# Border of two sublayers: `sqsum` statistics inside the last group, last chunk squared in two halves

## Chip, core and metric

The kernel runs on one core of a Trainium2 chip. The metric is the device time of one execution in microseconds; lower is better. Engines are named as in the profile: TensorE is PE (matmuls) and PEld (weight loads), VectorE is DVE, ScalarE is ACT, GpSimd is POOL, SyncE is SP, which issues the DMAs.

## What is computed

An encoder trunk of two layers on 512 tokens of width 1024, in float32. Every layer has an FFN, a token mixer (latent attention "MLA" in layer 0, gated recurrence "HGRN" in layer 1) and another FFN, so there are six sublayers. Each has an RMS norm at its entry and one at its end, before the residual addition:

```python
for l in range(DEPTH):
    g = norm_gains[l]
    x = x + 0.5 * rmsnorm(swiglu(rmsnorm(x, g[0]), ffn_w_in[l, 0], ffn_w_out[l, 0]), g[1])
    h = rmsnorm(x, g[2])
    m = mla(h, ...) if l % 2 == 0 else hgrn2(h, ...)
    x = x + rmsnorm(m, g[3])
    x = x + 0.5 * rmsnorm(swiglu(rmsnorm(x, g[4]), ffn_w_in[l, 1], ffn_w_out[l, 1]), g[5])
# rmsnorm(x, gain) = x * rsqrt(mean(x * x, axis=-1) + 1e-6) * gain
```

## The kernel before

All activations lie transposed: 1024 features as `KB` = 8 chunks of 128 partitions, 512 tokens as columns. A weight tile is 128x1024 (eight blocks of 128x128). Products are made exact enough by splitting both sides into a high and a low part: ScalarE rounds a tile (`w_hi`, L1339), GpSimd (L528) or VectorE (L1809) takes the rest (`w_lo`), and `mm3` issues three 128x512 matmuls for each block (L578 to L580). A group is one output chunk: 8 blocks for the up projection, the MLA output and the HGRN output, 22 blocks (`FB`) for the down projection of an FFN, each block three wide matmuls into one PSUM bank. Four weight slots form a ring; SP loads a slot (L453) when TensorE has released it through `w_free`.

The order of the work on each engine is written out by hand; waits are on semaphores and every engine runs its instructions in order. A sublayer ends with eight groups, output chunks 0 to 7 (`output_projection` on VectorE and ScalarE). For chunks 0 to 6, VectorE copies the group from PSUM into `y` (L1874), ScalarE squares the copy into `sq` (L1352, `square_y`), and VectorE adds the square to `sqsum` (L1882, L1885; signal `sq_added`). The last chunk is squared by ScalarE straight from PSUM (same line), and VectorE copies it only after that.

Then comes the border, of which there are six, the one after the last sublayer included. `post_statistics` on TensorE (L648) waits for seven `sq_added`, multiplies the four 128-token blocks of `sqsum` with a column of ones into PSUM bank `STAT` (L652; the first one releases the last weight slot, `close`), waits for the last square (`sq_ready`, L656) and adds the four products of `sq` (L658). ScalarE takes the root (L1357), VectorE the reciprocal (L1776), TensorE widens it over the partitions (L681), and VectorE normalises chunk after chunk and adds it to x (L1789, L1794); ScalarE forms `xg_hi` of each chunk (L1382), with which the next sublayer's first matmuls begin (L724). `keep_clock` (L675) fills waits with matmuls whose result is not used. At the FFN's end ScalarE runs one weight split (L1339) between the last square and the root, and after the first `xg_hi` it runs the split of the tile whose slot the last group held. At entry, `pre_statistics` (L668) makes four products of the same form as L652 in the middle of a group. TensorE's down projection is a loop of two turns with four groups each (L830).

## Time and profile before

| | us |
|---|---|
| median of 3 runs | 2062.91 (2062.24 to 2064.61) |
| profiled execution, its time | 2064.43 |
| profiled execution, its span | 2062.6 |
| PE busy | 2047.6 (99%) |
| DVE, ACT, POOL busy | 919.6, 713.2, 664.5 |

The span runs from the first to the last instruction of the program. Busy time is the union of the instructions' records; matmul records overlap, so the distance between two starts is the pace, not the length of one. "Idle before" is the time in which an engine stood still ahead of an instruction, with the engine and line that released it.

### The profile page before, as it was taken

What the parts mean: (1) busy time and instruction counts of PE and PEld (TensorE: products, weight loads), DVE (VectorE), ACT (ScalarE), POOL (GpSimd) and SP (SyncE); (2) the same over time, 40 slices, a digit from 0 to 9 for tenths busy, and PEclk for the clock granted to TensorE, in tenths of its full rate; (3) what the DMA queues carried; (4) which work ended last, traced back from release to release, by engine and by line L of the source; (5) the groups of instructions that cost most, each with busy time, mean ns of one, the idle gap of its engine ahead of it and who ended that gap; (6) DMA issues with size and microseconds to landing.
All of it is one profiled execution on the core that took longest, in us unless ns stands there. A gap on an engine that the chain in (4) does not pass through costs nothing.

```text
span 2062.6 us, 28297 instructions
## 1 busy us (share of the span) xinstructions
PE 2047.6 (99%) x11146; PEld 1676.7 (81%) x11146; DVE 919.6 (45%) x1223; ACT 713.2 (35%) x957; POOL 664.5 (32%) x286
## 2 busy tenths in 40 slices
PE   9999999999999999999999999999999999999998
PEld 7888888777888888888888888888888778888886
DVE  5434331668465334115543321466766775343212
ACT  4222232445342222223322222365655542222221
POOL 2444444230224444442444444200000014444442
PEclk9999999999999999999999999999999999999999
DMA  4332333310122323333223333222212122323332
GB/s 154 93 101 92 94 100 92 102 52 1 52 92 83 100 92 97 97 94 99 83 92 101 92 95 96 85 90 76 73 62 66 59 72 93 102 92 97 90 103 77
DMA packets 51634, 179.46 MB, mean 87 GB/s; under 512 B 5728, under 2 KB 5984, under 8 KB 51552
## 3 DMA queue, kind: packets, MB, share of 16 engines
q1 hardware_dynamic: 51552, 178.30, 27.5%
q8 instruction: 59, 0.97, 0.2%
q14 instruction: 23, 0.19, 0.0%
HBM read 176.18 MB, written 2.10 MB: 86 GB/s over the span
## 4 chain that ended last, share of the span: by engine, by line
PE 96%; DVE 2%; ACT 1%; issue 0%; DMA 0%; SPq 0%; DVEq 0%; ACTq 0%
PE psum L578 28%; PE psum L580 27%; PE psum L579 27%; PE psum L724 2%; PE psum L942 1%; PE psum L730 1%; PE psum L725 1%; PE psum L918 1%; PE psum L931 1%; PE psum L1048 1%; PE psum L681 0%; PE psum L750 0%; PE psum L757 0%; PE psum L754 0%; PE psum L1128 0%; PE psum L1085 0%
## 5 line engine op out<-in xcount | busy, mean ns | idle before, releaser
L528 POOL TENSOR_TENSOR w_lo<-raw,w_hi 128x1024 fp32r<-128x1024 f32 (+1 forms) x282 | 664.3, 2357 | 1370.0 <-ACT w_hi L1339 1370.0
L578 PE MATMUL psum<-xg_hi,w_hi 128*128 128x512 f32 x1735 | 688.8, 397 | 2.9 <-DVE xg_lo L2111 2.6
L580 PE MATMUL psum<-xg_hi,w_lo 128*128 128x512 f32 x1735 | 680.9, 392 | 0.0
L579 PE MATMUL psum<-xg_lo,w_hi 128*128 128x512 f32 x1735 | 675.5, 389 | 0.0
L1339 ACT ACTIVATE w_hi<-raw 128x1024 fp32r<-128x1024 f32 (+1 forms) x339 | 350.8, 1037 | 859.6 <-DMA raw<-w_up 471.6
L580 PEld LDWEIGHTS psum<-xg_hi,w_lo 128*128 128x128 f32 x1735 | 326.1, 188 | 75.2
L579 PEld LDWEIGHTS psum<-xg_lo,w_hi 128*128 128x128 f32 x1735 | 326.3, 188 | 70.4
L578 PEld LDWEIGHTS psum<-xg_hi,w_hi 128*128 128x128 f32 x1735 | 326.5, 188 | 69.6 <-DVE xg_lo L2111 2.9
L578 PE MATMUL psum<-hid_hi,w_hi 128*128 128x512 f32 x704 | 274.0, 389 | 0.0
L580 PE MATMUL psum<-hid_hi,w_lo 128*128 128x512 f32 x704 | 273.9, 389 | 0.0
L579 PE MATMUL psum<-hid_lo,w_hi 128*128 128x512 f32 x704 | 273.9, 389 | 0.0
L1853 DVE TENSOR_TENSOR t_b<-psum,r_pre 128x512 f32<-128x512 f32 x100 | 69.1, 691 | 348.3 <-PE psum L580 347.5
L1874 DVE COPY y<-psum 128x512 f32<-128x512 f32 x48 | 33.2, 692 | 402.4 <-PE psum L580 345.5
L578 PEld LDWEIGHTS psum<-hid_hi,w_hi 128*128 128x128 f32 x704 | 132.1, 188 | 27.5
L580 PEld LDWEIGHTS psum<-hid_hi,w_lo 128*128 128x128 f32 x704 | 132.1, 188 | 27.5
L579 PEld LDWEIGHTS psum<-hid_lo,w_hi 128*128 128x128 f32 x704 | 132.1, 188 | 27.5
L1860 DVE TENSOR_TENSOR t_d<-t_c,t_b 128x512 f32<-128x512 f32 x88 | 134.0, 1523 | 17.4 <-ACT t_c L1404 6.2
L1853 DVE TENSOR_TENSOR t_a<-psum,r_pre 128x512 f32<-128x512 f32 x100 | 69.1, 691 | 128.2 <-PE psum L580 107.8
L1404 ACT ACTIVATE t_c<-t_a 128x512 f32<-128x512 f32 x88 | 55.7, 633 | 127.2 <-DVE t_a L1853 127.2
L1809 DVE TENSOR_TENSOR w_lo<-raw,w_hi 128x1024 fp32r<-128x1024 f32 x57 | 69.7, 1223 | 12.6 <-ACT w_hi L1339 11.4
L1864 DVE TENSOR_TENSOR hid_lo<-t_d,hid_hi 128x512 f32 (+1 forms) x88 | 69.3, 788 | 9.4
L1885 DVE TENSOR_TENSOR sqsum<-sqsum,sq 128x512 f32<-128x512 f32 x36 | 43.1, 1198 | 32.5 <-ACT sq L1352 32.5
(233 smaller groups left out, 1595.4 us busy)
## 6 DMA issues: line engine op xcount, KB each, us to landing
raw<-w_up SPq DMA_DIRECT2D x176, 512.0 KB, 3.6
raw<-w_down SPq DMA_DIRECT2D x64, 512.0 KB, 3.5
raw<-w_hgrn SPq DMA_DIRECT2D x48, 512.0 KB, 3.6
raw<-w_down SPq DMA_DIRECT2D x32, 384.0 KB, 3.1
raw<-w_mla SPq DMA_DIRECT2D x19, 512.0 KB, 3.6
xt<-x_t SPq DMA_DIRECT2D x8, 256.0 KB, 6.4
out<-xt SPq DMA_DIRECT2D x8, 256.0 KB, 2.2
sq<-positions SPq DMA_DIRECT2D x1, 256.0 KB, 9.3
```

The costliest lines, as they stand in the source:

```text
L528: pool.tensor_tensor(w_lo[slot][:, 0:n], raw[slot][:, 0:n], w_hi[slot][:, 0:n].bitcast(F32), ALU.subtract).then_inc(w_ready, 1)
L578: first = pe.matmul(ps, w_hi[slot][:, at:at + n], hi, start=start, stop=False)
L579: pe.matmul(ps, w_hi[slot][:, at:at + n], lo, start=False, stop=False)
L580: return first, pe.matmul(ps, w_lo[slot][:, at:at + n], hi, start=False, stop=stop)
L724: first = pe.matmul(banks[g], w_hi[tiles[g]][:, at], xg_hi[:, k, :], start=k == 0, stop=False)
L1339: act.activation(w_hi[slot][:, 0:n], raw[slot][:, 0:n], ACT.Copy).then_inc(hi_made, 1)
L1404: act.activation(t_c[:, :], t_a[:, :], ACT.Silu).then_inc(silu_done, 1)
L1809: dve.tensor_tensor(w_lo[slot][:, :], raw[slot][:, :], w_hi[slot][:, :].bitcast(F32), ALU.subtract).then_inc(lo_made, 1)
L1853: dve.tensor_tensor(dst, bank(), r_pre[:, :], ALU.mult).then_inc(drained, 1)
L1860: dve.tensor_tensor(t_d[:, :], t_c[:, :], t_b[:, :], ALU.mult).then_inc(dve_step, 1)
L1864: dve.tensor_tensor(hid_lo[:, f, :], t_d[:, :], hid_hi[:, f, :].bitcast(F32), ALU.subtract).then_inc(hidden_ready, 1)
L1885: dve.tensor_tensor(sqsum[:, :], sqsum[:, :], src, ALU.add).then_inc(sq_added, 1)
```

## The change

Three edits. The products of `sqsum` leave `post_statistics` and become `sum_statistics`, which TensorE runs inside the last group of each sublayer: ahead of the last block of eight in MLA and HGRN, ahead of block 19 of 22 in an FFN; the wait for `sq_added` goes with them. The last chunk is squared in two instructions of 256 columns, each with its own signal, and the four products of `sq` wait for the first half ahead of the first and for the second half ahead of the third; the last slot is now released by the first of these. To place the products in the last group alone, TensorE's loop over the down projection is written out. VectorE's copy of the last chunk waits for both halves.

```diff
-            def group_into(ps, slot, hi, lo, middle=None, later=None):
+            def group_into(ps, slot, hi, lo, middle=None, later=None, final=None):
                 for k in range(KB):
+                    if final and k == KB - 1:
+                        final()
                     first, last = mm3(ps, (slot, k * P, P), hi[:, k, :], lo[:, k, :], k == 0, k == KB - 1)
...
-            def post_statistics():
+            def sum_statistics():
 
                 pe.wait_ge(sq_added, added.next(KB - 1))
                 for b in range(TB):
-                    first = pe.matmul(psum[:, STAT, b:b + 1], sqsum[:, b * P:(b + 1) * P], ones[:, 0:1],
-                                      start=b == 0, stop=False, skip_group_check=True)
+                    pe.matmul(psum[:, STAT, b:b + 1], sqsum[:, b * P:(b + 1) * P], ones[:, 0:1],
+                              start=b == 0, stop=False, skip_group_check=True)
+
+            def post_statistics():
+
+                for b in range(TB):
                     if b == 0:
-                        close(first)
-                pe.wait_ge(sq_ready, squared.next(KB))
-                for b in range(TB):
+                        pe.wait_ge(sq_ready, squared.next(KB))
+                    elif b == TB // 2:
+                        pe.wait_ge(sq_ready, squared.next())
                     last = pe.matmul(psum[:, STAT, b:b + 1], sq[:, (KB - 1) % 2, b * P:(b + 1) * P], ones[:, 0:1],
                                      start=False, stop=b == TB - 1, skip_group_check=True)
+                    if b == 0:
+                        close(last)
                 last.then_inc(stat_done, 1)
...
-                with loop(pe, KB // 4, (ready, 4 * len(DOWN_PARTS)), (bank_free, 4), stream=stream):
+                for i in range(KB // 4):
                     for j in range(4):
...
+                                if f == FB - 3 and i * 4 + j == KB - 1:
+                                    sum_statistics()
...
-                for _ in range(2, KB):
-                    group_into(open_next(), open_tile(), xg_hi, xg_lo)
+                for j in range(2, KB):
+                    slot = open_tile()
+                    group_into(open_next(), slot, xg_hi, xg_lo, final=sum_statistics if j == KB - 1 else None)
...
-                project(by_dve=False)
+                slot = open_tile()
+                group_into(open_group(LONG_RING), slot, xg_hi, xg_lo, final=sum_statistics)
...
-                    src = psum[:, ends[0], :]
+                    for at in (slice(0, SEQ // 2), slice(SEQ // 2, SEQ)):
+                        act.activation(sq[:, j % 2, at], psum[:, ends[0], at], ACT.Square).then_inc(sq_ready, 1)
+                    return
...
-                        dve.wait_ge(sq_ready, squared.next())
+                        dve.wait_ge(sq_ready, squared.next(2))
```

## Rows read from the trace of the kernel before

**Rows 1.** The page: engines' busy time, and the chain that ended last.
```profile
PE 2047.6 (99%) x11146; PEld 1676.7 (81%) x11146; DVE 919.6 (45%) x1223; ACT 713.2 (35%) x957; POOL 664.5 (32%) x286
PE 96%; DVE 2%; ACT 1%; issue 0%; DMA 0%; SPq 0%; DVEq 0%; ACTq 0%
```

**Rows 2.** Timeline, first border: start us, length us, engine, line, operands, [idle before].
```profile
374.67 0.39 PE L580 MATMUL psum<-hid_hi,w_lo 128*128 128x512 f32 x1
374.67 1.08 PEld L652 LDWEIGHTS psum<-const,sqsum 128*128 128x128 f32 x8
375.15 0.60 ACT L1352 ACTIVATE sq<-psum 128x512 f32<-128x512 f32 x1 [4.80 <-PE psum L580]
375.65 1.05 ACT L1339 ACTIVATE w_hi<-raw 128x1024 fp32r<-128x1024 f32 x1
375.80 1.05 PE L658 MATMUL psum<-const,sq 128*128 128x1 f32 x8
376.89 0.26 ACT L1357 ACTIVATE root<-psum,eps 128x4 f32<-128x4 f32 x1 [0.20 <-PE psum L658]
380.34 1.04 ACT L1339 ACTIVATE w_hi<-raw 128x1024 fp32r<-128x1024 f32 x1
```

**Rows 3.** Timeline, second border, after the MLA layer.
```profile
578.00 0.60 ACT L1352 ACTIVATE sq<-psum 128x512 f32<-128x512 f32 x1 [0.71 <-PE psum L580]
579.74 0.26 ACT L1357 ACTIVATE root<-psum,eps 128x4 f32<-128x4 f32 x1 [1.14 <-PE psum L658]
```

**Rows 4.** Timeline, `pre_statistics` (L668) inside a group at the entry of MLA.
```profile
405.22 0.40 PE L580 MATMUL psum<-xg_hi,w_lo 128*128 128x512 f32 x1
405.45 0.95 PE L668 MATMUL psum<-const,sqsum 128*128 128x1 f32 x8
406.26 0.48 PE L578 MATMUL psum<-xg_hi,w_hi 128*128 128x512 f32 x1
406.58 0.39 PE L579 MATMUL psum<-xg_lo,w_hi 128*128 128x512 f32 x1
```

**Rows 5.** ScalarE, a group by form (busy us, mean ns), and a timeline row.
```profile
L1608 ACT ACTIVATE state<-psum 128x256 f32<-128x256 f32 x8 | 3.1, 383 | 7.7 <-PE psum L1106 7.7
...
1485.16 1.52 ACT L1591 ACTIVATE near<-psum 32x256 f32<-32x256 f32 x4
```

**Rows 6.** Timeline, border after the HGRN layer.
```profile
1676.85 1.34 DVE L1885 TENSOR_TENSOR sqsum<-sqsum,sq 128x512 f32<-128x512 f32 x1 [0.76 <-ACT sq L1352]
1677.26 0.39 PE L578 MATMUL psum<-xg_hi,w_hi 128*128 128x512 f32 x1
1678.24 0.97 PEld L652 LDWEIGHTS psum<-const,sqsum 128*128 128x128 f32 x8 [0.56 <-DVE sqsum L1885]
1678.66 1.28 SPq L453 DMA_DIRECT2D raw<-w_up  x3
1679.16 1.03 PE L658 MATMUL psum<-const,sq 128*128 128x1 f32 x8
1680.23 0.26 ACT L1357 ACTIVATE root<-psum,eps 128x4 f32<-128x4 f32 x1 [1.42 <-PE psum L658]
```

**Rows 7.** Timeline, last addition to `sqsum` in the first FFN and in MLA.
```profile
361.65 1.13 DVE L1885 TENSOR_TENSOR sqsum<-sqsum,sq 128x512 f32<-128x512 f32 x1 [0.76 <-ACT sq L1352]
...
573.96 0.79 DVE L1885 TENSOR_TENSOR sqsum<-sqsum,sq 128x512 f32<-128x512 f32 x1 [0.76 <-ACT sq L1352]
```

**Rows 8.** L453 at the first border: ns min/median/max, first and last start; landing us.
```profile
L453 SPq DMA_DIRECT2D raw<-w_mla x3: 328/430/432, 375.2 to 376.1; - x3
...
DMA to landing us min/median/max: 3.8/4.7/5.5
```

**Rows 9.** Timeline, TensorE at the end of the down loop's first turn.
```profile
314.83 0.39 PE L580 MATMUL psum<-hid_hi,w_lo 128*128 128x512 f32 x1
315.06 0.39 PE L578 MATMUL psum<-hid_hi,w_hi 128*128 128x512 f32 x1
```

**Rows 10.** A stretch: us; busy PE, PEld, DVE, ACT, POOL; PEclk, DMA share, GB/s.
```profile
1618.00:1621.40 3.40, 2.69 (x6) 2.15 (x7) 3.33 (x6) 1.00 (x2) 0.00 (x0) 0.59 0.05 18
```

## Prediction

> **What bounds the kernel now.** I read the page first: TensorE is busy in 99% of the span and the chain that ended last is 96% TensorE [rows 1]. So whatever is added to TensorE's stream counts in full, and other engines count only where TensorE waits for them. That happens at the six borders, where a sublayer's output is normalised and each new chunk of x needs the previous result. The second view is the timeline of the first border [rows 2]. Let A be the start of the squaring of the last chunk there, 375.15. The last wide matmul starts 0.48 before A. The reader should see two things run side by side after it. ScalarE squares 512 columns in 0.60 and the square is usable at 375.75. TensorE meanwhile does the four `sqsum` products (eight passes, since each fp32 product is recorded as two), and these have been issued at 375.75 too (374.67 + 1.08). At 375.80 the four products with `sq` begin, at 376.89 the root. So the `sqsum` products have hardly any price at present: the squaring covers them. From A to the root it is 1.74, at this border, where a weight split stands in between, and at the second, where none does [rows 3].
>
> **The change part by part.** Times are us.
>
> 1. *Four `sqsum` products move into the last group.* The nearest row is the same work in the same place: `pre_statistics` in the middle of a group [rows 4]. Without it a matmul follows every 0.23, so after the L580 at 405.22 an L578 would start at 405.45 and an L579 at 405.68. With the eight passes the L579 starts at 406.58. The cost is 406.58 - 405.68 = 0.90 of TensorE's own time. Ends: 0.81, if only the gap from first pass to next wide matmul is counted (406.26 - 405.45), and 0.90, which I take, as the L578 behind them is itself stretched. Nothing hides it, since the group's end, and A with it, come 0.90 later. I call the new start A'.
>
> The Trainium skill (TensorE: Matmul & The Clock Gate, LDWEIGHTS) gives a weight load 128/1.2 = 107 ns; eight would be an estimated 0.85 by that page, and the sum 0.3 smaller over six borders. The trace measures the pair and decides.
>
> 2. *Squaring in two halves.* No row shows a half square, but ScalarE took 383 ns for 256 columns out of PSUM [rows 5] where 512 took 0.60. So the first half is ready at A' + 0.38 and TensorE starts at A' + 0.43, with the 0.05 between a ScalarE end and TensorE's start that 375.75 to 375.80 shows. The second half: four 256-column reads of PSUM by L1591 took 1.52 together, hence 0.38 each without overlap [rows 5]; it ends at A' + 0.77 and is usable at A' + 0.82. The third product is due at A' + 0.43 + 4 x 0.113 = A' + 0.88 (0.113 is eight passes in 0.90), so the second wait is just covered, by 0.06. If it were not, each 0.1 of lateness costs 0.1 per border.
>
> 3. *Root.* From the first of the `sq` passes to the root it is now 376.89 - 375.80 = 1.09. When TensorE starts them from idle, eight passes took 0.92 rather than 0.90 (1678.24 to 1679.16 [rows 6]), so 1.11. Root at A' + 0.43 + 1.11 = A' + 1.54 against A + 1.74: a gain of 0.20. The engine is left idle after the wide matmuls where it had the moved products to do, so only this 0.20 of the 0.90 returns. At the three FFN borders that have a sublayer behind them, ScalarE runs a weight split of 1.05 between square and root [rows 2]. It would start 0.10 before the second half's end, as it does now (375.65 against 375.75), and end at A' + 1.72. If the root follows with the same overlap it comes at A' + 1.63, the gain there being 0.11; without it 0.01, and 0.20 if the halves overlap too. I take 0.11, as the overlap is what the rows show between square and split.
>
> Five borders so far: 3 x (0.90 - 0.11) + 2 x (0.90 - 0.20) = 2.37 + 1.40 = 3.77.
>
> The Trainium skill (ScalarE: Activation LUTs, Rules for kernel authors) speaks against halves: about 0.3 us per instruction and 0.83 ns per element. By an estimate from it the halves would end at A' + 0.51 and A' + 1.02, the third product would wait, and the gain would fall from 0.20 to about 0.1. The rows show 0.383 for 256 columns, smaller than that, so I stay with the rows.
>
> 4. *The new wait on `sq_added`.* It stands in TensorE's in-order stream, so the last chunk's matmuls, and everything after, queue behind it. In an FFN `sqsum` is complete at 361.65 + 1.13 = 362.78, and the products stand three blocks of 3 x 0.23 before the end of the wide matmuls at 374.9 [rows 2], some ten us later [rows 7]. In the MLA layer it is complete at 573.96 + 0.79 = 574.75, and the last chunk's matmuls start 0.48 + 2 x 0.23 before 578.00, at 577.06 [rows 3, 7]: 2.3 to spare. In the HGRN layer VectorE is behind: `sqsum` is complete at 1678.19, but the last chunk's matmul starts at 1677.26 [rows 6]. Today the wait stands after that chunk and costs 0.56. Moved before it, the products start at 1678.24, the last chunk's first matmul at 1678.24 + 0.92 - 0.09 = 1679.07 (0.09 is 0.90 less 0.81, from part 1), its second 0.32 later (406.26 to 406.58) and its third 0.23 after that, 1679.62. A' = 1680.10, root 1680.10 + 1.54 = 1681.64 against 1680.23 now: +1.41. Bounds: +0.70, if `sqsum` came in time, and +1.9.
>
> 5. *`close` moves.* The last weight slot is released by the first `sq` product, not the first `sqsum` product. Now the load is issued at A + 0.05 (375.2) and lands 3.8 later [rows 8]. From an idle start, issue follows 0.42 after the first pass (1678.24 to 1678.66 [rows 6]), so it will be at A' + 0.43 + 0.42 = A' + 0.85 and land at A' + 4.65. SP's two loads queued behind it shift likewise, but are needed only at chunks 4 and 6. ScalarE needs the slot in its split after the first chunk, 380.34, which is 3.45 after the root [rows 2], so at A' + 4.99 to A' + 5.08. Hidden, with 0.3 to 0.4 to spare; without that cover each 0.1 costs 0.1 at five borders.
>
> 6. *The loop over the down projection is written out* on TensorE. At the end of its first turn (315.06) the matmuls keep their 0.23 [rows 9]: nothing to gain. For a loss the straight-line code of the MLA layer (405.22 to 405.45 [rows 4]) shows the same 0.23. I take 0.
>
> 7. VectorE's copy of the last chunk now waits for both halves, begins at A' + 0.82 and ends 0.69 later, before the root ends. 0.
>
> **Sum**: 3.77 + 1.41 = +5.2. The profiled execution has a span of 2062.6 and took 2064.43, so it would become 2069.6; it lies 1.5 above the median of the runs, 2062.91, to which I add the same 5.2: **2068.1**, or 0.25% slower.
>
> **Rivals.**
>
> *Ra, the moved products hide under wide matmuls (not slower).* If their weight loads were pulled under the wide matmuls and a pass of one column took next to nothing, the 0.90 would vanish, and with the gains of 3 x 0.11 + 2 x 0.20 and an HGRN border at +0.5 the result is 2062.91 - 0.7 + 0.5 = 2062.7. With a price p in the group the sum is 6p - 0.2 (5.2 at 0.90), so the change is within 0.2%, 4.1, from p below 0.72. Against it: [rows 4] show 0.90 for exactly this case. The Trainium skill (TensorE: Matmul & The Clock Gate, opening table) says that this engine pulls weight loads ahead of running matmuls, which would favour it; the pass rate of [rows 4] already contains what that saves. Chance 3%.
>
> *Rb, the late slot.* The three loads at the first border landed in 3.8 to 5.5 [rows 8], the first in 3.8. If it took 4.5, ScalarE's split would be late by 0.4, and the next chunk's `xg_hi` behind it. Over five borders +2.0: 2070.1. It decides from a landing over 4.1. Chance 12%.
>
> *Rc, the HGRN wait is small.* The add that ends late took 1.34 where the same instruction took 0.79 in the MLA layer [rows 6, 7]; were it 0.79, `sqsum` would be ready 0.55 earlier: 2067.5. Nothing here changes what runs beside it. Chance 8%.
>
> *Rd, the clock.* In one stretch of 3.4 in the HGRN layer, in which TensorE was busy for 2.69, the granted clock was 0.59 of full speed, partly at the lower of the two levels (1.2 instead of 2.4 GHz) [rows 10]. The change adds some 0.7 of idle time at each border. One more such stretch, on wide matmuls, costs at most 3.4 x 0.41 = 1.4: 2069.5. It decides if a stretch behind a border shows less than 0.9. Chance 10%.
>
> *Re, the halves bring nothing* (root at A' + 1.74 everywhere): +5 x 0.90 + 1.6 = 6.1, 2069.0. Chance 7%.
>
> **How the numbers follow.** The forecast has 60% and an own range of 4.3 (0.81 per border, all gains 0.20, HGRN +1.2) to 6.1 (no gains). The runs of before scatter from 2062.24 to 2064.61, some 0.7 below and 1.7 above the median. The range from 2066.0 to 2070.8 takes in the forecast, Rc, Re, most of Rb and Rd, and leaves out Ra. A difference of 0.2%, about what a measurement can tell from no change here, is 4.1, so slower needs 2067.0. Of the forecast's 60% about 47 lie above it; with Rb, Rd, Re and a part of Rc that is 0.77 for slower. Same: 0.20, from the rest and most of Ra. Faster by more than that: 0.03, as no case gives it and only unmodelled effects could.
>
> **What the profile after would show.** Right: in the last group L652's eight passes, next wide matmul pair 0.90 late; two squares of about 0.38; the first L658 pass 0.43 after the square's start; roots at A' + 1.54 to 1.63; at the HGRN border TensorE idle for almost 1 before L652. Wrong: wide matmuls at an unbroken 0.23 around the products, a second half later than A' + 0.88, a root that waits for the split, an `xg_hi` of the second chunk that waits behind a split which waits for its load or a granted clock under 0.9 behind a border.

## The result and the profile after

| | before | after |
|---|---|---|
| median of 10 runs, us | 2063.06 | 2069.35 |
| lowest to highest | 2062.24 to 2064.97 | 2068.12 to 2073.28 |
| ratio | | 1.0031 [1.0023, 1.0039] |
| profiled execution, time | 2064.43 | 2073.28 |
| its span | 2062.6 | 2071.5 |
| its mean granted clock | 0.997 | 0.995 |

The change makes the kernel slower by 6.3 us. The profiled execution of after is the slowest of the ten, so its span overstates the difference (8.9); a later series of eleven runs gave 2069.3 against 2063.86, ratio 1.0028 [1.0019, 1.0037], that is 5.4. The trace of that series serves here as a second one of the same kernel.

The page of after shows the picture of [rows 1] again. TensorE is busy 99% of the time, with the same number of matmuls in 5.9 us more.

```profile
PE 2053.5 (99%) x11146; PEld 1680.9 (81%) x11146; DVE 896.0 (43%) x1223; ACT 713.3 (34%) x963; POOL 664.2 (32%) x286
```

**In the last group.** The timeline of TensorE in the third sublayer (an FFN), with the columns of [rows 2]; it answers to [rows 4]. The moved products have line L654 now.

```profile
949.70 0.39 PE L580 MATMUL psum<-hid_hi,w_lo 128*128 128x512 f32 x1
949.93 0.95 PE L654 MATMUL psum<-const,sqsum 128*128 128x1 f32 x8
950.74 0.48 PE L578 MATMUL psum<-hid_hi,w_hi 128*128 128x512 f32 x1
951.05 0.39 PE L579 MATMUL psum<-hid_lo,w_hi 128*128 128x512 f32 x1
```

From the L580 to the L579 it is 1.35. With the usual step of 0.227 and nothing in between it would be 0.45, so the products cost 0.90, as step 1 of the prediction has it. That distance is 1.35 to 1.37 at every insertion in every trace, except in the HGRN layer, where a wait is added (below).

**An FFN border.** The border of the same sublayer, the third (A' = 953.12), in the timeline of all engines, in the form of [rows 2]:

```profile
953.12 0.66 ACT L1364 ACTIVATE sq<-psum 128x256 f32<-128x256 f32 x2 [5.88 <-PE psum L580]
953.56 1.05 PE L664 MATMUL psum<-const,sq 128*128 128x1 f32 x8 [0.53 <-ACT sq L1364]
953.67 1.06 ACT L1351 ACTIVATE w_hi<-raw 128x1024 fp32r<-128x1024 f32 x1
953.98 1.28 SPq L453 DMA_DIRECT2D raw<-w_up  x3
954.65 0.26 ACT L1371 ACTIVATE root<-psum,eps 128x4 f32<-128x4 f32 x1
954.81 2.35 POOL L528 TENSOR_TENSOR w_lo<-raw,w_hi 128x1024 fp32r<-128x1024 f32 x1 [5.09 <-ACT w_hi L1351]
956.66 1.05 DVE L1808 SCALAR_TENSOR_TENSOR xt<-t_a,half_cols,xt 128x512 f32<-128x512 f32 x1
957.74 0.72 ACT L1396 ACTIVATE xg_hi<-xt,cols 128x512 fp32r<-128x512 f32 x1 [2.83 <-DVE xt L1808]
```

And the same border of before, where the last square starts at A = 947.74:

```profile
947.74 0.60 ACT L1352 ACTIVATE sq<-psum 128x512 f32<-128x512 f32 x1 [4.72 <-PE psum L580]
...
949.36 2.36 POOL L528 TENSOR_TENSOR w_lo<-raw,w_hi 128x1024 fp32r<-128x1024 f32 x1 [3.88 <-ACT w_hi L1339]
...
951.49 0.78 DVE L1794 SCALAR_TENSOR_TENSOR xt<-t_a,half_cols,xt 128x512 f32<-128x512 f32 x1
...
952.30 0.72 ACT L1382 ACTIVATE xg_hi<-xt,cols 128x512 fp32r<-128x512 f32 x1 [2.56 <-DVE xt L1794]
```

Read each start from its own A. The root is at 1.53 instead of 1.74: the gain is there, 0.21. But the first `xg_hi`, which TensorE needs, starts at 4.62, against 4.56 before. The gain is gone between root and `xg_hi`, and the row that shows where is the last VectorE instruction before it: it starts at 3.54 instead of 3.75 but takes 1.05 instead of 0.78, and ends no sooner than before.

**The MLA border** (A' = 581.32), and two stretches of the view that gives busy time and granted clock, with the columns of [rows 10]:

```profile
581.32 0.66 ACT L1364 ACTIVATE sq<-psum 128x256 f32<-128x256 f32 x2 [1.91 <-PE psum L580]
581.76 1.42 PE L664 MATMUL psum<-const,sq 128*128 128x1 f32 x8 [0.53 <-ACT sq L1364]
583.22 0.26 ACT L1371 ACTIVATE root<-psum,eps 128x4 f32<-128x4 f32 x1 [1.23 <-PE psum L664]
...
586.64 0.72 ACT L1396 ACTIVATE xg_hi<-xt,cols 128x512 fp32r<-128x512 f32 x1 [3.16 <-DVE xt L1808]
```

```profile
580.40:582.30 1.90, 1.37 (x9) 0.88 (x8) 0.19 (x1) 0.66 (x2) 1.45 (x1) 1.00 0.00 0
582.30:589.10 6.80, 6.80 (x22) 5.62 (x21) 4.41 (x8) 2.64 (x5) 0.00 (x0) 0.50 0.64 233
```

Here the first `xg_hi` starts 5.32 after the square, against 4.54 before. Up to 1.0 after A' the clock was granted in full, with TensorE busy for 1.37 of 1.90; then it is 0.50, the lower of the two levels, 1.2 GHz. The passes with `sq` take 1.42 instead of 1.05 together and the root comes at 1.90.

**The HGRN border** (A' = 1686.11), timeline and stretch; it answers to [rows 6]:

```profile
1682.77 1.33 DVE L1899 TENSOR_TENSOR sqsum<-sqsum,sq 128x512 f32<-128x512 f32 x1 [0.76 <-ACT sq L1366]
1683.75 0.39 PE L580 MATMUL psum<-xg_hi,w_lo 128*128 128x512 f32 x1
1684.15 1.05 PE L654 MATMUL psum<-const,sqsum 128*128 128x1 f32 x8
1685.07 0.48 PE L578 MATMUL psum<-xg_hi,w_hi 128*128 128x512 f32 x1
1685.38 0.40 PE L579 MATMUL psum<-xg_lo,w_hi 128*128 128x512 f32 x1
...
1686.11 0.66 ACT L1364 ACTIVATE sq<-psum 128x256 f32<-128x256 f32 x2 [3.38 <-PE psum L580]
...
1690.90 0.72 ACT L1396 ACTIVATE xg_hi<-xt,cols 128x512 fp32r<-128x512 f32 x1 [3.00 <-DVE xt L1808]
```

```profile
1688.20:1691.60 3.40, 3.36 (x10) 2.92 (x11) 2.12 (x3) 0.70 (x2) 0.00 (x0) 0.50 0.97 343
```

`sqsum` is complete at 1684.10, 0.12 after the moment at which the products could have begun (1683.75 + 0.23), and they begin at 1684.15: a wait of 0.17, where the prediction had 0.98. The insertion costs more than its 0.90 and this wait, though: from the L580 to the L579 it is now 1.63, and 1.63 less 0.45 is 1.18. The other 0.11 is that TensorE starts the products from a standstill: the next wide matmul follows 0.92 after the first pass (1684.15 to 1685.07) instead of 0.81 (949.93 to 950.74). So the HGRN layer pays 0.28 on top of the 0.90. The clock falls 2.1 after A', and `xg_hi` is at 4.79 against 4.82 before.

**Where the span's 8.9 went.** Cut at the starts of the last square, the two executions differ section by section. "Step" is what the rows above give for a section: 0.90 for its insertion, plus the change from square to `xg_hi` at the border with which it begins.

| section | before | after | difference | step | left over |
|---|---|---|---|---|---|
| start to 1st square | 375.15 | 374.67 | -0.48 | 0.90 | -1.38 |
| to 2nd (MLA) | 202.84 | 206.65 | +3.81 | 0.90 + 0.05 | +2.86 |
| to 3rd | 369.74 | 371.80 | +2.06 | 0.90 + 0.78 | +0.38 |
| to 4th | 368.96 | 369.91 | +0.95 | 0.90 + 0.05 | 0.00 |
| to 5th (HGRN) | 361.51 | 363.08 | +1.57 | 0.90 + 0.05 + 0.28 | +0.34 |
| to 6th | 369.24 | 370.41 | +1.17 | 0.90 - 0.03 | +0.30 |
| to the end | 15.19 | 14.98 | -0.21 | -0.20 | -0.01 |

The steps sum to 6.4, close to the median's difference of 6.3; the same terms read from the second trace of after give 5.8, against 5.4. The -1.38 has a likely source in the clock early in the first FFN: before has a granted clock of 0.50 from 10.9 to 14.3, where after has 1.00. Over all traces the first square of a last chunk lies between 373.2 and 376.3 (377.6 in the kernel with slower matmuls of experiment 6), and the two highest below that are the two traces with such a stretch, before (375.15) and the second one of after (376.33). Most of the 2.86 lies in a stretch at the entry of the MLA layer, ahead of any edit of that layer:

```profile
404.80:411.60 6.80, 6.80 (x26) 5.92 (x25) 2.19 (x8) 1.64 (x4) 2.36 (x1) 0.50 0.00 0
```

In the second trace of after that section is 203.79, +0.95 over before, as the steps have it.

### The profile page after: what moved, and what is told of

Its sections match the earlier page's. It is cut to its first block, busy times and chain, and to the rows that moved or that the text cites. A ratio compares the mean times of both kernels' runs of the same rounds, so it can differ in the third digit from the quotient of the medians.

```text
span 2071.5 us, 28179 instructions
## 1 busy us (share of the span) xinstructions
PE 2053.5 (99%) x11146; PEld 1680.9 (81%) x11146; DVE 896.0 (43%) x1223; ACT 713.3 (34%) x963; POOL 664.2 (32%) x286
## 4 chain that ended last, share of the span: by engine, by line
PE 97%; DVE 2%; ACT 1%; issue 0%; DMA 0%; SPq 0%; DVEq 0%; ACTq 0%
PE psum L578 28%; PE psum L580 27%; PE psum L579 27%; PE psum L732 1%; PE psum L952 1%; PE psum L733 1%; PE psum L738 1%; PE psum L928 1%; PE psum L941 1%; PE psum L1059 1%; PE psum L689 1%; PE psum L683 0%; PE psum L765 0%; PE psum L762 0%; PE psum L1139 0%; PE psum L1117 0%
## 5 line engine op out<-in xcount | busy, mean ns | idle before, releaser
L578 PE MATMUL psum<-xg_hi,w_hi 128*128 128x512 f32 x1735 | 689.8, 398 | 2.9 <-DVE xg_lo L2125 2.6
L580 PE MATMUL psum<-xg_hi,w_lo 128*128 128x512 f32 x1735 | 681.1, 393 | 0.0
L579 PE MATMUL psum<-xg_lo,w_hi 128*128 128x512 f32 x1735 | 675.9, 390 | 0.0
L580 PEld LDWEIGHTS psum<-xg_hi,w_lo 128*128 128x128 f32 x1735 | 326.2, 188 | 75.7
L579 PEld LDWEIGHTS psum<-xg_lo,w_hi 128*128 128x128 f32 x1735 | 326.7, 188 | 70.1
L578 PEld LDWEIGHTS psum<-xg_hi,w_hi 128*128 128x128 f32 x1735 | 326.8, 188 | 69.7 <-DVE xg_lo L2125 2.9
L578 PE MATMUL psum<-hid_hi,w_hi 128*128 128x512 f32 x704 | 274.3, 390 | 0.0
L580 PE MATMUL psum<-hid_hi,w_lo 128*128 128x512 f32 x704 | 273.9, 389 | 0.0
L579 PE MATMUL psum<-hid_lo,w_hi 128*128 128x512 f32 x704 | 273.9, 389 | 0.0
L580 PEld LDWEIGHTS psum<-hid_hi,w_lo 128*128 128x128 f32 x704 | 132.1, 188 | 27.6
L579 PEld LDWEIGHTS psum<-hid_lo,w_hi 128*128 128x128 f32 x704 | 132.2, 188 | 27.4
L578 PEld LDWEIGHTS psum<-hid_hi,w_hi 128*128 128x128 f32 x704 | 132.1, 188 | 27.3
L1874 DVE TENSOR_TENSOR t_d<-t_c,t_b 128x512 f32<-128x512 f32 x88 | 111.2, 1264 | 17.4 <-ACT t_c L1418 6.2
L1823 DVE TENSOR_TENSOR w_lo<-raw,w_hi 128x1024 fp32r<-128x1024 f32 x57 | 69.7, 1223 | 13.1 <-ACT w_hi L1351 12.0
```

The source lines that it names most:

```text
L578: first = pe.matmul(ps, w_hi[slot][:, at:at + n], hi, start=start, stop=False)
L579: pe.matmul(ps, w_hi[slot][:, at:at + n], lo, start=False, stop=False)
L580: return first, pe.matmul(ps, w_lo[slot][:, at:at + n], hi, start=False, stop=stop)
L1823: dve.tensor_tensor(w_lo[slot][:, :], raw[slot][:, :], w_hi[slot][:, :].bitcast(F32), ALU.subtract).then_inc(lo_made, 1)
L1874: dve.tensor_tensor(t_d[:, :], t_c[:, :], t_b[:, :], ALU.mult).then_inc(dve_step, 1)
```

## The experiments

All times are in us; each ratio is against runs of the kernel before on the same chip. "From A" is from the start of the last square of the border. Expected texts name lines and quantities as the prediction does.

**1. The parts alone.** The unrolled loop alone, on the kernel before:

```diff
-                with loop(pe, KB // 4, (ready, 4 * len(DOWN_PARTS)), (bank_free, 4), stream=stream):
+                for i in range(KB // 4):
```

> The kernel before with TensorE's loop over the down projection written out and nothing else. Theory: no difference (within 0.3). Rival (instruction fetch of the longer straight program): the part of the measured +6.3 that the borders don't explain, 0.5 to 1, is already here, with gaps between wide matmuls of the down projections.

Measured: 2062.01, ratio 0.9995 [0.9986, 1.0003]. The wide matmuls keep their 0.23 with either form. Step 6 (nothing) holds. One thing changes that the prediction doesn't name: VectorE's busy time falls from 919.6 to 896.3 with the same 1223 instructions, 22 of it at one line (L1860, 1523 ns down to 1270 each). Why was not looked into; VectorE is not what bounds the kernel there, and the time stays.

The halves alone, with the products of `sqsum` at their old place:

```diff
-                    src = psum[:, ends[0], :]
+                    for at in (slice(0, SEQ // 2), slice(SEQ // 2, SEQ)):
+                        act.activation(sq[:, j % 2, at], psum[:, ends[0], at], ACT.Square).then_inc(sq_ready, 1)
+                    return
```
```diff
                 for b in range(TB):
+                    if b == TB // 2:
+                        pe.wait_ge(sq_ready, squared.next())
...
```

> The kernel before with the two half squares and the wait for the second one ahead of the third product; the sqsum products stay at the border and the loop stays. Theory: no difference (within 0.3), since TensorE issues the sqsum products until 0.64 after the square's start anyway and the first sq product can't come earlier: root at 1.74. Rival (the square, not the products, was the bound): root at 1.54, up to -1.2 in all.

Measured: 2062.8, ratio 0.9996 [0.9987, 1.0005]. The timeline of its third border:

```profile
945.89 0.66 ACT L1354 ACTIVATE sq<-psum 128x256 f32<-128x256 f32 x2 [4.83 <-PE psum L580]
946.44 1.03 PE L660 MATMUL psum<-const,sq 128*128 128x1 f32 x8
...
947.50 0.26 ACT L1361 ACTIVATE root<-psum,eps 128x4 f32<-128x4 f32 x1
947.57 2.34 POOL L528 TENSOR_TENSOR w_lo<-raw,w_hi 128x1024 fp32r<-128x1024 f32 x1 [4.04 <-ACT w_hi L1341]
949.51 0.95 DVE L1798 SCALAR_TENSOR_TENSOR xt<-t_a,half_cols,xt 128x512 f32<-128x512 f32 x1
950.49 0.72 ACT L1386 ACTIVATE xg_hi<-xt,cols 128x512 fp32r<-128x512 f32 x1 [2.72 <-DVE xt L1798]
```

The passes with `sq` begin at 0.55 after A instead of 0.65, so the `sqsum` passes ahead of them are through by 0.55: before, it was the square alone that came last, by 0.10. The halves thus gain 0.12 in the root even without the move (1.62), where the expectation had none (1.74) and its rival 0.20: of the 0.21 that the whole change gains in the root, the move adds only 0.09. Again VectorE's instruction is long (0.95), and `xg_hi` is at 4.60. At the MLA border of this kernel, where GpSimd has no split, the same instruction takes 0.75 and `xg_hi` is at 4.41 instead of 4.54.

The move alone, with one square of 512 columns:

```diff
-                    for at in (slice(0, SEQ // 2), slice(SEQ // 2, SEQ)):
-                        act.activation(sq[:, j % 2, at], psum[:, ends[0], at], ACT.Square).then_inc(sq_ready, 1)
-                    return
+                    src = psum[:, ends[0], :]
```

> The sqsum products move into the last group as in the change (loop written out too), but the last chunk is squared in one instruction of 512 columns. Theory: 0.92 per border (0.90 in the group, and the sq products start from an idle TensorE) at five borders and 1.6 at HGRN: +6.2 against the kernel before; the root comes 1.76 after the square's start. The residual instruction of chunk 0 is not stretched, as root and GpSimd's split lie as before, so this is only 0.5 slower than the changed kernel, although the root itself is 0.2 later at six borders (1.2). Rival (halves pay in full): 1.2 slower than the changed kernel.

Measured: 2071.02, ratio 1.0031 [1.0019, 1.0042]. At the third border:

```profile
951.24 0.60 ACT L1362 ACTIVATE sq<-psum 128x512 f32<-128x512 f32 x1 [5.75 <-PE psum L580]
...
954.98 0.77 DVE L1804 SCALAR_TENSOR_TENSOR xt<-t_a,half_cols,xt 128x512 f32<-128x512 f32 x1
955.79 0.72 ACT L1392 ACTIVATE xg_hi<-xt,cols 128x512 fp32r<-128x512 f32 x1 [2.55 <-DVE xt L1804]
```

The root is at 1.74 and `xg_hi` at 4.55, with VectorE's instruction at 0.77: everything from A on is as before, and the insertion of 0.90 comes on top. At the MLA and HGRN borders the clock falls 1.1 and 1.3 after A, and `xg_hi` is at 5.63 and 5.43. The loss belongs to the move; in time the halves give almost nothing back. The expectation put this kernel 0.5 behind the full change and its rival 1.2; 2071.02 is 1.7 behind the 2069.30 of the same series, but with intervals that overlap, so the times don't choose between them. Two things are left to explain: the price at the FFN borders, and the lower clock.

**2. The HGRN wait.** The products go back behind the group in the HGRN layer only:

```diff
-                group_into(open_group(LONG_RING), slot, xg_hi, xg_lo, final=sum_statistics)
+                group_into(open_group(LONG_RING), slot, xg_hi, xg_lo)
+                sum_statistics()
```

> The changed kernel with the sqsum products of the HGRN layer back behind its last group; the other five borders as changed. Theory: the HGRN layer wins back 0.90 for the products and 0.1 to 0.3 of waiting, and its root comes at 1.62 instead of 1.53: 1.0 below the changed kernel. Rival (my prediction's price of the new wait, 0.98): 1.8 below.

Measured: 2067.24, ratio 1.0024 [1.0014, 1.0035], against 1.0031 and 1.0028 for the full change, so 0.8 to 1.4 less by the ratios; their intervals overlap, and the time doesn't decide between the expected 1.0 and the rival's 1.8. The trace does. At this border of its trace:

```profile
1680.14 0.66 ACT L1365 ACTIVATE sq<-psum 128x256 f32<-128x256 f32 x2 [2.03 <-PE psum L580]
1681.76 0.26 ACT L1372 ACTIVATE root<-psum,eps 128x4 f32<-128x4 f32 x1 [0.96 <-PE psum L664]
...
1684.56 0.72 ACT L1397 ACTIVATE xg_hi<-xt,cols 128x512 fp32r<-128x512 f32 x1 [2.53 <-DVE xt L1809]
```

The root is at 1.62 and `xg_hi` at 4.42, and the granted clock is full throughout. With the move it was 4.79 after a wait of 0.17. The wait itself was small in each trace with the products moved there: 0.17, 0.07, 0.27, 0.09, 0.19 and 0.04 (after, after again, the move alone, the idle filled, experiment 5, only the mixers), with 0.11 for the standstill on top each time. Its size depends on how far VectorE is behind. In before its last addition ends 0.93 after the start of the first of the last three wide matmuls (1678.19 less 1677.26, [rows 6]); in the six other traces with the products behind the group this is 0.44, 0.39, 0.28, 0.21, 0.01, and -0.33 with the unrolled loop alone, an edit that does nothing in this layer. So the 0.93 was the high end of a scatter.

**3. Idle time as the cause of the clock.** The first theory for the clock at those borders was the idle time between the wide matmuls and the `sq` products. One `keep_clock` matmul pair at the head of `post_statistics` fills it:

```diff
             def post_statistics():
 
+                keep_clock(1)
                 for b in range(TB):
```

> The changed kernel with one more keep-clock matmul (two passes of 256 columns) ahead of the first sq product, in the 0.7 in which TensorE stands idle there. Theory (the idle stretch ahead of the products is what lets the clock fall early in the border): root still 1.53 after the square's start; no stretch at the lower clock begins before 2.4 after it, so the first xg_hi of the FFN layers after MLA and HGRN comes 4.34 to 4.41 after the square's start instead of 4.79, and the time is 0.9 below the changed kernel. Rival (where the clock falls is chance): as the changed kernel, 4.79.

Measured: 2069.63, ratio 1.0033 [1.0022, 1.0045], as slow as after. Timeline and stretch at the HGRN border:

```profile
1682.43 0.59 PE L684 MATMUL psum<-const 128*128 128x256 f32 x2
1682.69 0.66 ACT L1365 ACTIVATE sq<-psum 128x256 f32<-128x256 f32 x2 [3.38 <-PE psum L580]
...
1687.48 0.72 ACT L1397 ACTIVATE xg_hi<-xt,cols 128x512 fp32r<-128x512 f32 x1 [3.00 <-DVE xt L1809]
```
```profile
1684.20:1687.60 3.40, 3.40 (x11) 2.60 (x12) 1.74 (x4) 0.38 (x2) 0.00 (x0) 0.50 0.89 317
```

The gap is filled, yet the clock falls 1.5 after A and `xg_hi` is at 4.79. At the MLA border of this one trace it didn't fall. So the idle gap is not needed for the clock to fall. Whether filling it makes the fall rarer, two borders with one result each way can't say.

**4. Place by place.** The move at the FFN borders only, that is experiment 2 with the MLA border put back too:

```diff
-                    group_into(open_next(), slot, xg_hi, xg_lo, final=sum_statistics if j == KB - 1 else None)
+                    group_into(open_next(), slot, xg_hi, xg_lo)
+                sum_statistics()
```

> The changed kernel with the sqsum products of MLA and HGRN back behind their last groups; only the four FFN layers keep them inside. Theory by the terms measured so far: 4 x 0.90 in the groups, +0.05 at three FFN borders, -0.22 at the last, -0.13 at the borders after MLA and HGRN: +3.3 against the kernel before, 2.6 below the changed kernel: 1.9 for two groups and HGRN's wait, the rest because the clock stays up at the borders after MLA and HGRN (first xg_hi at 4.41, not 4.79 or 5.2). Rival (the lower clock there has nothing to do with the moved products): the stretches at the lower clock begin 1.0 to 2.1 after the square's start here too.

Measured: 2065.45, ratio 1.0013 [1.0004, 1.0022]. The reverse, the move at MLA and HGRN only:

```diff
-                                if f == FB - 3 and i * 4 + j == KB - 1:
-                                    sum_statistics()
...
+                sum_statistics()
```

> The counterpart of ffn_only: the sqsum products stay inside the last group in MLA and HGRN and go back behind it in the four FFN layers; halves and the written-out loop stay. Theory: 2 x 0.90 in the groups and 0.1 to 0.3 of waiting in HGRN; the two borders behind start their products at 0.44 after the square, but the clock falls 1.0 to 2.1 after it at both, so the first xg_hi comes at 4.8 to 5.4 (+0.3 to +0.9 against 4.54); FFN borders +0.05 with the root at 1.62, last border -0.12. Sum +2.5 to +4. Rival (the clock falls by chance and not because of the moved products): no stretch begins before 2.4 after the square at these two borders, first xg_hi at 4.34, sum +1.6.

Measured: 2066.85, ratio 1.0020 [1.0011, 1.0029]. The stretches behind the MLA border (first) and the HGRN border (second) in the FFN kernel, with the products unmoved there:

```profile
577.00:582.00 5.00, 4.90 (x31) 3.94 (x30) 2.88 (x5) 1.50 (x4) 1.41 (x1) 1.00 0.62 207
1678.20:1683.20 5.00, 4.90 (x31) 3.91 (x30) 2.91 (x5) 1.51 (x4) 0.00 (x0) 1.00 0.58 204
```

and in the mixers' kernel, with the products moved there (A is 576.96 and 1678.50):

```profile
578.10:581.50 3.40, 3.40 (x13) 2.88 (x13) 1.38 (x4) 0.26 (x1) 0.00 (x0) 0.50 0.79 264
1680.60:1684.00 3.40, 3.38 (x10) 2.93 (x11) 2.13 (x3) 0.71 (x2) 0.00 (x0) 0.50 0.93 359
```

The columns before the last three are TensorE, its weight loads, VectorE, ScalarE, GpSimd; the third from the right is the clock. The kernel with the halves alone, 0.9996, is what each differs from by its insertions. Four insertions at FFN borders (the one at the end included) cost (1.0013 - 0.9996) x 2063 = 3.5, or 0.9 each; two at the mixers cost (1.0020 - 0.9996) x 2063 = 5.0, or 2.5 each. By the intervals each of the two differences is uncertain by about 2.6, so 0.9 +- 0.7 against 2.5 +- 1.3. The insertion is 0.90 at both places, and the rest is what the mixers' place adds; the medians lean that way, but the two intervals touch. The rows of the mixers' kernel give 3.1 for its two, inside its 5.0 +- 2.6: insertions of 0.90 and 1.05, and `xg_hi` 0.74 and 0.38 later than with the halves alone. The mean clock over the runs agrees: 0.9981 for the FFN kernel and 0.9973 for before in its series, 0.9958 for the mixers' kernel and 0.9976 for before in its series.

Over all traces, at the MLA and HGRN borders:

| | borders | clock at 0.50 within 3 of A | begins after A |
|---|---|---|---|
| products inside the last group | 13 | 12 | 1.0 to 2.1 |
| products behind it | 13 | 3 | 2.4 to 2.9 |

Four of the 13 borders with the products behind the group are of experiment 6, with half as many passes; none of those fell, so with passes like the others it is 3 of 9. Of 39 FFN borders the clock falls at two, 2.4 (the halves alone) and 3.0 (the move alone) after A, though 21 of them have the products in the last group too.

What it costs depends on when it begins: up to 1.3 after A `xg_hi` is at 5.15 to 5.63, 0.8 to 1.1 late against an undisturbed border with the same squares (4.32 in the MLA layer of experiment 3 with the halves, 4.54 with one square); from 1.5 to 2.1 it is 4.79, or 0.47 late; at 2.4, 0.4 to 0.5; at 2.9 nothing.

**5. What holds VectorE at the FFN borders.** GpSimd's split runs beside that instruction at 36 borders of twelve traces. At 35 of them the instruction ends 0.55 after the split's end, whenever it starts:

| | split starts, ends from A | VectorE starts | takes | ends |
|---|---|---|---|---|
| before | 1.62, 3.98 | 3.75 | 0.78 | 4.52 |
| halves alone | 1.68, 4.02 | 3.63 | 0.95 | 4.58 |
| after | 1.68, 4.03 | 3.53 | 1.04 | 4.58 |
| experiment 6 | 1.68, 4.03 | 3.50 | 1.08 | 4.58 |

The 36th is the fourth border of the halves alone, where the lower clock makes it start late: at 3.91, with the split again over at 4.03, it takes 0.75 and ends at 4.66. All 36 fit one formula: it ends at the later of its start + 0.75 and the split's end + 0.55.

If GpSimd holds it, a split that is over sooner must set it free. So for the three sublayers that follow an FFN sublayer (`s` of 1, 3 and 4, counted from 0) the entry tile in question gets one block of the split instead of eight:

```diff
-                for _ in range(ENTRY - 1):
-                    split()
+                for t in range(ENTRY - 1):
+                    split(1 if s in (1, 3, 4) and t == ENTRY - 2 else 8)
...
```

The kernel leaves out the low part of that tile's weights: its products take `w_hi` where `w_lo` stood, so the number of matmuls is the same.

> The changed kernel, with GpSimd's weight split behind the three FFN borders cut to 128 of 1024 columns (0.3 instead of 2.35); the low part of that tile is left out, and TensorE multiplies its high part in its place, so TensorE's work is the same. Theory (GpSimd's split stretches the residual instruction of chunk 0 there): that instruction falls from 1.05 to 0.75 at the three borders, the first xg_hi comes 4.31 to 4.36 after the square's start instead of 4.61, and the time is 0.8 below the changed kernel. Rival (something else holds VectorE): 1.05 and 4.61 stay.

At its third border:

```profile
948.74 0.66 ACT L1370 ACTIVATE sq<-psum 128x256 f32<-128x256 f32 x2 [5.74 <-PE psum L582]
...
950.42 0.45 POOL L528 TENSOR_TENSOR w_lo<-raw,w_hi 128x128 fp32r<-128x128 f32 x1 [4.95 <-ACT w_hi L1357]
952.28 0.75 DVE L1814 SCALAR_TENSOR_TENSOR xt<-t_a,half_cols,xt 128x512 f32<-128x512 f32 x1
953.06 0.72 ACT L1402 ACTIVATE xg_hi<-xt,cols 128x512 fp32r<-128x512 f32 x1 [2.53 <-DVE xt L1814]
```

GpSimd is done at 2.13, VectorE's instruction takes 0.75, and `xg_hi` is at 4.32 instead of 4.62, at all three borders. That shows the cause: with the split out of the way the hold is gone. The Trainium skill (SBUF — State Buffer, "SBUF: two separate sides") describes it: VectorE with two inputs in SBUF and a GpSimd operation that reads SBUF share a pair of ports, and whichever started first holds it for its whole instruction. The rows agree that VectorE waits for GpSimd's end; but an instruction that began only then and took its full 0.75 would end 0.2 later than the 4.58 seen, so the first 0.20 of it doesn't seem to need what GpSimd holds. In time: 2068.26, ratio 1.0022 [1.0012, 1.0031], where 3 x 0.30 = 0.9 less than after was due. 1.0028 or 1.0031 less 0.0004 is 1.0024 or 1.0027, so the median fits, but the intervals overlap and the trace, not the time, carries this.

**6. Cheaper products instead of moved ones.** If the product of one column costs two passes because it is fp32, fp32r operands should need one. `sqsum`, the last `sq` and the column of ones become fp32r, on the kernel with the halves alone; a product then has two equal columns, of which the root reads the first:

```diff
-                    first = pe.matmul(psum[:, STAT, b:b + 1], sqsum[:, b * P:(b + 1) * P], ones[:, 0:1],
+                    first = pe.matmul(psum[:, STAT, 2 * b:2 * b + 2], sqsum_r[:, b * P:(b + 1) * P], ones_r[:, 0:2],
...
```

The edit changes the precision of the statistics: the last term of `sqsum` and the last square are rounded to fp32r.

> The kernel before with two half squares, and with sqsum (its last addition), the last square and the ones rounded to the fp32r type, so that each product of the post and entry statistics is one pass (two equal columns, as one column doesn't compile) and not two; the products stay where they were before. Theory: the six entry statistics inside groups take 0.45 instead of 0.90 (-2.7). At a border the sqsum passes end early and the four sq passes take 0.45: root 1.08 to 1.1 after the square's start at the borders after MLA, HGRN and the last one (-0.65 each); at the three FFN borders ScalarE's weight split holds the root until 1.5 and GpSimd's split eats the rest (0). Sum -4.6. Rival (a pass costs the same whatever its type, and there are still eight per statistic): no change.

Measured: 2081.85, ratio 1.0092 [1.0076, 1.0107]. The border gained what was expected, but the wide matmuls of the whole kernel had become slower. The groups of instructions show it (busy us, mean ns):

```profile
L581 PE MATMUL psum<-xg_lo,w_hi 128*128 128x512 f32 x1735 | 686.1, 395 | 0.0
```

That line had 389 before and its two fellows grew as well, the busy times of the three by 18.7 together; the groups with `hid` stayed at 389. What differs is addresses. The new array of 8 bytes a partition, rounded up to 32 in the program as built, had been placed ahead of the weight slots and of `hid` and shifts both by 32 bytes; `xg` is allocated ahead of it and did not move. So the matmuls that became slower are those in which the weights moved and the activations did not, and with `hid`, where both moved alike, nothing changed. The second version allocates the array behind all of them:

```diff
-        ones_r = sb("ones_r", [P, 2], F32R)
...
         ring_at = slab("ring", RING * 2 * TILE * 4)
+        ones_r = sb("ones_r", [P, 2], F32R)
```

> As one_pass, with the two columns of ones placed behind the weight slots, so that no other tile's address moves by 8 bytes. Theory (in one_pass the moved addresses of weights and activations cost the wide matmuls of the up projections 4 to 6 ns each, 19 in all, and hid the gain): -4.4 against the kernel before: entry statistics 6 x 0.45, borders after MLA and HGRN and the last one 0.6 each (first xg_hi 3.95 after the square's start), FFN borders +0.05. Rival (the fp32r statistics themselves slow the matmuls): again some 19 slower.

Measured: 2058.53, ratio 0.9975 [0.9966, 0.9984], faster than both kernels. L581's group is back at 389. The timeline of the MLA border:

```profile
576.48 0.66 ACT L1356 ACTIVATE o_first<-psum 128x256 fp32r<-128x256 f32 x2 [0.83 <-PE psum L582]
...
577.61 0.26 ACT L1366 ACTIVATE root<-psum,eps 128x4 f32<-128x4 f32 x1 [0.47 <-PE psum L662]
...
580.43 0.72 ACT L1391 ACTIVATE xg_hi<-xt,cols 128x512 fp32r<-128x512 f32 x1 [2.55 <-DVE xt L1803]
```

Root at 1.13 and `xg_hi` at 3.95, 0.59 before the 4.54 of the kernel before. The entry's `pre_statistics` takes 0.45 in a group instead of 0.90, six times: 2.7. MLA 0.59, HGRN 0.87 (4.82 to 3.95) and the end 0.60 (15.19 to 14.59) make 2.06, the FFN borders nothing, since GpSimd's split holds them at 4.62 (4.56 in before). Together 4.8, against 5.3 on the median. Of the 0.87, 0.28 is VectorE's lateness in the one trace of before (`xg_hi` at 4.82 where 4.54 is the value without it), so 4.5 is the steadier sum. The halves are part of this kernel too, so the 5.3 is not the price of the passes alone.

**7. The change once more**, to have a second trace and a larger number of runs:

> The changed kernel once more, unaltered, for a second trace of it. Theory: time is +5.7 without disturbances of TensorE's clock (3 FFN borders at 0.95, since behind the root the first residual instruction runs beside GpSimd's weight split and is stretched from 0.78 to 1.05, which takes back the 0.20 of the halves; MLA and last border 0.70 each; HGRN 1.4), plus some tenths to some us where the granted clock is at its lower level behind a border. Rival (clock alone): the stretched instruction is chance, the FFN borders cost 0.70 to 0.79 each in this trace, and all that lies above +5.2 comes from stretches at the lower clock. In the trace: length of the residual instruction of chunk 0 behind the borders, and the stretches at the lower clock.

Measured: 2069.3, ratio 1.0028 [1.0019, 1.0037]. The first `xg_hi` is at 4.61 at the FFN borders and at 4.79 at both the MLA and the HGRN border, where the clock falls 2.0 and 1.7 after A.

## Why the prediction came out as it did

The forecast was 2068.1, in a range of 2066.0 to 2070.8, and "slower". The time is 2069.35: direction and range held, and the sum of +5.2 was 1.1 short of +6.3 (0.2 short of the +5.4 of the second series). The direction is earned: the 0.90 of step 1 at six places carries it. That the number came so close is in part luck, since errors of both signs stand behind it: HGRN 0.73 too much without the clock, the FFN borders 0.48 too little, and the clock, left out of the sum, 0.98 at the MLA and 0.47 at the HGRN border. -0.73 + 0.48 + 0.98 + 0.47 = +1.2, which is the 6.4 of the rows less 5.2.

| term | predicted | shown |
|---|---|---|
| insertion, six times | 0.90 | 0.90 |
| root, FFN borders | -0.11 | -0.21 |
| `xg_hi`, FFN borders | as the root | +0.05 each |
| MLA border, square to `xg_hi` | -0.20 | +0.78 (4.79 again: +0.25) |
| HGRN border in all | +1.41 | +1.15 (0.90 + 0.28 - 0.03) |
| end | 0.90 - 0.20 | 0.90 - 0.21 |

- *Step 1*, the price in the group, is right at all places, taken from the same work in the same surroundings.
- *Step 2* has the root right (A' + 1.54; measured 1.53), and the wait on the second half covered, though the halves do overlap by 0.10: two of 385 and 377 ns take 0.66, so the second starts at 0.28. That pulls the weight split ahead as well (0.54 instead of 0.67) and gives the FFN borders the full 0.21. The estimate from the Trainium skill that stood against the halves (ScalarE: Activation LUTs, Rules for kernel authors) used about 0.3 us per instruction; the page states this for a bias given as a pointer operand, which the squares don't have (`sq<-psum` reads nothing else), and the rows show 0.38 for 256 columns.
- *Step 3* is the step that failed. It let the gain in the root stand as a gain for TensorE. At the FFN borders another gate closes behind the root: the GpSimd split that holds VectorE's instruction until 4.58. The earlier root arrives at a closed gate, and because the halves put the weight split, and with it GpSimd's, 0.05 later (1.62 to 1.68), the border ends 0.05 later too. In the rows of before the hold is just visible: 0.77 at this instruction, where 0.75 is its length without a neighbour, and it was the timeline of GpSimd that I didn't follow. The cost is 3 x 0.16 = 0.5 against the forecast. Experiment 5 shows this. A second thing in this step: it credits the earlier root to the change as a whole, and experiment 1 shows that 0.12 of the 0.21 needs no move; the 0.90 bought 0.09.
- *Step 4* has the mechanism right and the size wrong: 1.15 in all where +1.41 was due. The wait is 0.04 to 0.27, not 0.98, because VectorE's lag at this place varies from execution to execution by more than 1 (-0.33 to 0.93) and the profiled one had it longest. It also reads the price of today's wait wrongly: the 0.56 in [rows 6] is idle time of the weight loads, while TensorE's next matmul was due three steps after the L578, at 1677.26 + 3 x 0.23 = 1677.95, and began at 1678.24, so that the wait cost 0.29 (the root of before is at 2.02 there, against 1.74 elsewhere). Rival Rc had put this at 8%, for another reason (a shorter addition; it still takes 1.33). Without the clock the border would have been 0.90 + 0.28 - 0.50 = +0.68 (4.82 to 4.32).
- *Step 5* is right: the loads are issued 0.85 after A' (953.98 less 953.12 is 0.86), the first landed 3.2 to 3.9 later, and no split waits for it. Rival Rb did not occur. *Steps 6 and 7*: nothing, as forecast.
- *Rival Rd*, the clock, held 10% and is what took place, at two borders rather than one. The rival's reason, the added idle time, is not supported as the only cause: with the gap filled the clock at the HGRN border still fell (experiment 3).

What the clock reacts to is left open. Shown is the place: 12 of 13 borders with the products inside the mixers' last group, 3 of 13 with the products behind it. By the medians a kernel with the move at these places alone loses more than one with the move at the FFN borders alone (1.0020 against 1.0013), but these intervals overlap, and the times don't show it. At the mixers the moved products stand only one block, 0.68, before the end of the group, at the FFN borders three blocks, 2.04; so one-column passes, idle time and one-column passes again lie closer together there. A version with the products three blocks ahead in the mixers, which would test that, was not run, so this is a guess.

## What to carry to other kernels

Work that stands under a wait costs nothing; moved into the stream of the bounding engine it costs its full length (0.90 here), and only what it kept from starting comes back (0.09 in the root here; the other 0.12 came from the halves, and without them the move brought nothing back). Follow a gain at one gate through to the next consumer on the bounding engine, with every neighbour that can hold up an engine in the chain: a VectorE instruction whose length differs from that of its twins is the sign. And make small products cheaper before moving them: half the passes, with the halves, gave 5.3 where the move with the halves lost 6.3. About half of that gain (2.7) was made at the entry of the sublayers, a place that the change never touched.

## What the runs showed that was not expected

- A VectorE operation with two SBUF inputs that starts beside a GpSimd operation ends 0.55 after that one's end (0.75 alone; 0.78, 0.95, 1.04 and 1.08 beside it), unless it starts so late that its own 0.75 ends later still (3.91 + 0.75 = 4.66).
- Two squares of 256 columns out of PSUM, back to back, take 0.66 together where one of 512 takes 0.60; the second starts 0.28 after the first.
- An fp32 product with one column is two passes of 113 ns each in a stream; an fp32r product with two columns is one (four in 0.45).
- A shift of the weight slots by 32 bytes a partition, with `xg` left where it was, made the wide matmuls that read `xg` longer (389 to 395 ns recorded for L581's group) and cost about 19 us of 2063. With `hid`, which shifted along, they kept their 389. The one line moved between the two versions shows that it is the placement; which relation of the addresses matters was not tested.
- The granted clock can fall to 0.50 right behind a stretch in which TensorE was busy for 1.37 of 1.90 (MLA border of after), and, with no edit near, at the entry of MLA (404.80 to 411.60 in after): in four of the seven traces with products in the FFN layers' last groups, and in one of the six others. Whether the move has a part in that is open.
